# Row products and value rounds of a product-key expert layer dealt anew over the stages of a two-layer decoder step

## The reference, cut to what matters

```python
for li in range(2):                       # layer 0: RWKV-7 time mixing, layer 1: gated linear attention
    x = x + gt1 * mixer(rmsnorm(x) * (1 + sc1) + sh1)
    h = rmsnorm(x) * (1 + sc2) + sh2
    x = x + gt2 * peer(h)                 # product-key experts
...
def block(xt):                            # peer, for every token
    q = (xt @ wq).reshape(PEER_BLOCK, PEER_HEADS, 2, PEER_HALF)
    s = jnp.einsum('thpk,hpnk->thpn', q, subkeys)
    ...                                   # the 16 best of 128 keys on each side, then the 16 best of their 256 sums
    ue = jnp.take(u, expert, axis=0)      # 8 heads x 16 experts: 128 rows of 1024 numbers for every token
    act = gelu(jnp.einsum('thed,td->the', ue, xt))
    ve = jnp.take(v, expert, axis=0)
    return jnp.einsum('the,thed->td', gate * act, ve)
```

## Time and profile before

| | |
|---|---|
| time, three runs | 3379.37, 3380.48 (median), 3386.27 us |
| profiled execution | 3384.7 us, its span 3382.9 us |
| granted TensorE clock | 0.748 of full |
| TensorE matmul busy | 1900.9 us, 56% |
| VectorE busy | 1643.6 us, 49% |
| GpSimd busy | 1318.5 us, 39% |
| ScalarE busy | 267.7 us, 8% |
| HBM read | 816.05 MB, 244 GB/s over the span |

### The profile page before, as it was taken

One profiled execution on the slowest core, in us unless ns is written; L12 is line 12 of the kernel. 1 busy time (PEld: TensorE's weight loads), 2 busy tenths in 40 slices (PEclk: granted clock), 3 DMA queues, 4 the chain that ended last, 5 costly groups with the idle time before them and its releaser, 6 DMA issues.

```text
span 3382.9 us, 24243 instructions
## 1 busy us (share of the span) xinstructions
PE 1900.9 (56%) x8947; PEld 1081.7 (32%) x8947; DVE 1643.6 (49%) x3011; ACT 267.7 (8%) x422; POOL 1318.5 (39%) x1160
## 2 busy tenths in 40 slices
PE   4889648457786244565756576456255771004426
PEld 1377523125553212332314333443223360000002
DVE  3354486771221868752312522677943158880033
ACT  1111000100000000010000010011110000000000
POOL 0000026663332066433402620057664224775564
PEclk8989869578777666677878787778578885556668
DMA  7421349996567289657856943379789655998897
GB/s 240 172 92 53 129 161 397 340 339 231 187 199 261 102 324 321 217 174 253 303 190 259 392 159 129 118 269 360 262 307 357 232 193 189 355 342 309 305 312 256
DMA packets 296706, 827.99 MB, mean 245 GB/s; under 512 B 45951, under 2 KB 57135, under 8 KB 296589
## 3 DMA queue, kind: packets, MB, share of 16 engines
q0 software_dynamic: 165888, 604.05, 50.1%
q1 hardware_dynamic: 120132, 218.02, 18.4%
q10 hardware_dynamic: 10568, 4.38, 0.5%
HBM read 816.05 MB, written 10.31 MB: 244 GB/s over the span
## 4 chain that ended last, share of the span: by engine, by line
PE 35%; DVE 20%; DMA 20%; POOL 12%; issue 9%; ACT 2%; another core or an unknown queue 1%; SPq 1%; DVEq 0%; ACTq 0%; POOLq 0%; PEldq 0%
PE psum L1663 33%; POOL arena L583 12%; DVE arena L908 6%; DMA arena<-in_peer_v,idx_v 5%; DVE arena L925 4%; DMA arena<-in_peer_u,idx_u 4%; DMA wring<-in_gla_w_in 3%; DMA wring<-in_ada_w 2%; DMA wring<-in_rw_wo 1%; DVE arena L1043 1%; DVE arena L1046 1%; DVE arena L1044 1%; ACT arena L624 1%; DMA hT<-in_state_rwkv_S 1%
## 5 line engine op out<-in xcount | busy, mean ns | idle before, releaser
L583 POOL DMA_INDIRECT arena<-in_peer_u,idx_u x576 | 748.9, 1300 | 1089.1 <-DVEq L1478 617.2
L1663 PE MATMUL psum<-arena 128*32 128x512 f32 (+5 forms) x4226 | 819.0, 589 | 466.0 <-DMA arena<-in_peer_v,idx_v 160.5
L925 DVE CUSTOM_DVE_ANT_0 arena<-arena,hc 128x1024 f32<-128x1024 f32 x576 | 689.4, 1224 | 397.0 <-DMA arena<-in_peer_u,idx_u 351.8
L583 POOL DMA_INDIRECT arena<-in_peer_v,idx_v x512 | 502.7, 982 | 839.0 <-PE psum L1663 711.3
L1663 PEld LDWEIGHTS psum<-arena 128*128 128x128 f32 (+2 forms) x4226 | 397.0, 174 | 830.8 <-issue 585.6
L1663 PE MATMUL psum<-wring,cT 128*9 128x512 f32 x384 | 196.0, 671 | 129.4 <-DMA wring<-in_ada_w 128.5
L1663 PE MATMUL psum<-hT,wring 128*128 128x128 f32 (+3 forms) x1824 | 233.9, 291 | 22.6 <-DMA wring<-in_gla_w_in 14.3
L1663 PE MATMUL psum<-wring,hT 128*128 128x512 f32 x384 | 189.8, 656 | 87.5 <-DMA wring<-in_rw_wo 40.4
L1663 PEld LDWEIGHTS psum<-hT,wring 128*128 128x128 f32 (+1 forms) x1824 | 223.2, 196 | 40.9 <-issue 20.5
L624 ACT ACTIVATE arena<-psum 128x512 f32<-128x512 f32 (+5 forms) x143 | 109.2, 764 | 1248.9 <-PE psum L1663 951.7
L1663 PE MATMUL psum<-wring,arena 128*128 128x512 f32 (+1 forms) x312 | 149.5, 636 | 36.8 <-DMA wring<-in_rw_g 17.3
(11 more groups left out here) (195 smaller groups left out, 1528.9 us busy)
## 6 DMA issues: line engine op xcount, KB each, us to landing
wring<-in_ada_w SPq DMA_DIRECT2D x24, 2048.0 KB
wring<-in_peer_wq SPq DMA_DIRECT2D x20, 2048.0 KB
wring<-in_rw_w_rkv SPq DMA_DIRECT2D x12, 2048.0 KB
wring<-in_gla_w_in SPq DMA_DIRECT2D x12, 2048.0 KB
wring<-in_rw_wo SPq DMA_DIRECT2D x6, 2048.0 KB
vring<-mod_d SPq DMA_DIRECT2D x22, 512.0 KB
arena<-in_peer_u,idx_u POOLq DMA_INDIRECT x576
arena<-in_peer_v,idx_v POOLq DMA_INDIRECT x512
```

Source lines behind the costliest of these rows:

```text
L583: pool.indirect_dma_start(ring[:, s, :], None, v_rows if side else u_rows, bass.IndirectOffsetOnAxis(index, 0)).then_inc(rows_landed[s], 16)
L925: dve.tensor_tensor_reduce(ring[:, s, :], ring[:, s, :], hc[:, t, :], 1.0, 0.0, MUL, ADD, acts[:, (3 * li + t) % 2, col:col + 1]).then_inc ...
L1663: return nc.tensor.matmul(out, lhsT, rhs, start=start, stop=stop)
```

## The change

The deal of the expert work over the stages is changed; no arithmetic is.

- TensorE: `serve()` is taken out of `for_vector` and `for_scalar`; it stays in `operands()`, with higher rates (4 rounds a wait, 1.1 in `gla(0)`). In `out`, up to 6 and 4 rounds are put ahead of the two waits for chosen experts. `rest_values` at the end of `out` is kept in layer 1 alone.
- Phase 00: 28 u rows in `mix((1,2))` at its two places (rate 14), 12 after it (`rest_rows(24)`), 24 in the head of `core(1)`; the other 64 in `core(1)`'s halves (1.9 a place). `weights_due` of the first half moves into `core(1)`, that of the second to its end, and the value rounds open after that: 4 at the wait for `stateT`, 4 ahead of `turn(y)`, 4, 6 and 4 in `out(0,(1,))`, and the last 10 ahead of the first `modulation` of `core(2)`.
- Phase 01: 64 u rows in each half of `core(2)` (2.6 a place); value rounds from the end of `core(2)` on: 4, 4 and 4 at waits up to `gla_mixer((0,))`, 12 in `gla(0)`, 8 after it. `add_experts(0, 1)` moves behind `gla(0)`.
- Phase 02: u rows in `out(1,(0,))` (7 a place), `weights_due` between the first two key blocks and the first `choose`, value rounds ahead of the waits for chosen experts.
- Phase 10: u rows 6 at the norm's wait, then as before up to 64, and the other 64 at 1.6 a place in `gla(1)` and `gla(2)`; the value rounds open after `gla(2)`: 4, 6, 4, and 18 at the end of `out(1,(1,2))`.
- SyncE's loads of the gate vector (`mod_vec(0, 5)`) move with `add_experts`.

```diff
                 if t:
                     if sample:
-                        mod_vec(0, 5)
                         sp.wait_ge(region_free, w.next(region_free))
...
                 if sample:
+                    mod_vec(0, 5)
                     for hh in range(2):
...
+            RATES = {"mix": 14, "core1": 1.9, "core2": 2.6, "enter": 6, "gla": 1.6, "out": 7}
...
-                if t:
-                    weights_due(0, t - 1, 1 if t == 1 else 0)
+                if t == 1:
+                    weights_due(0, 0, 0)
+                    open_rows(0, 0, 64, 64, RATES["core1"])
                 if sample:
-                    open_rows(0, 1, 64, 64, 3.2)
+                    add_experts(0, 0, zz)
+                    open_rows(0, 1, 0, 64, RATES["core2"])
...
-                weights_due(*((0, SAMPLE) if tiles[0] == 0 else (1, 0, 0)))
-                if tiles[0]:
-                    open_rows(1, 0, 64, 64, 2.2)
+                    weights_due(1, 0, 0)
+                    open_rows(1, 0, 64, 64, RATES["gla"])
                 for t in tiles:
                     gla(t, tiles)
-                    if t == 1:
-                        weights_due(1, 0, 1)
+                if tiles[0]:
+                    weights_due(1, 0, 1)
+                else:
+                    add_experts(0, 1, add_tmp)
...
+                if li and tiles[0] == 0:
+                    open_rows(0, SAMPLE, 0, SHORT, RATES["out"])
...
+                    if li and t == 0 and half == 0:
+                        weights_due(0, SAMPLE)
...
-            open_rows(0, 0, 0, 64, 20)
+            open_rows(0, 0, 0, 64, RATES["mix"])
             mix((1, SAMPLE))
-            weights_due(0, 0, 0)
-            open_rows(0, 0, 64, 64, 8)
+            rest_rows(24)
...
+            VALUE_RATES = {"out": 4, "gla": 1.1}
...
             def for_vector():
-                serve()
...
             def for_scalar(cols=D):
-                serve()
...
                 for _ in PREP_MODS[t]:
+                    if sample:
+                        rest_values()
                     modulation()
...
                 if t == 1:
+                    fan_weights(0, 0, 1)
+                    banks.two = False
+                    open_values(0, 0, VALUE_RATES["out"])
                     operands()
...
                 if tiles[0] < SAMPLE:
                     for half in range(2):
+                        for _ in range(min(stream.left, 6 - 2 * half)):
+                            stream.left -= 1
+                            value_round()
                         pe.wait_ge(operand_written, w.next(operand_written))
                         fan_out(e1[:, 64 * half:64 * half + 64], 64)
-                rest_values()
+                if li:
+                    rest_values()
```

More of the change, by code:

```diff
@@ L520, in _ @@
                     vec(row("gla_gnorm"))
+                if tiles[0] == 0:
+                    mod_vec(0, 5)
                 if tiles[0]:
@@ L730, in core @@
                     if not group[0]:
-                        if t:
-                            weights_due(0, t - 1, 1 if t == 1 else 0)
                         if t == 1:
-                            banks.two = False
+                            weights_due(0, 0, 0)
                         for li, k in PREP_MODS[t]:
@@ L764, in core @@
                             nst[i] += 16
-                    if hh == 0:
-                        weights_due(0, 1, 1)
+                    weights_due(0, 1, hh)
                     for i in range(2):
@@ L770, in core @@
                 if t == 1:
+                    weights_due(0, 0, 1)
+                    banks.two = False
                     copy_out(state_out[0][0:RK, :], D, RK)
@@ L791, in out @@
                 t = tiles[0]
+                if li and t == 0:
+                    weights_due(0, SAMPLE, 0)
                 for half in (range(2) if t < SAMPLE else ()):
@@ L854, in gla_mixer @@
                 act.sem_inc(scalar_result, 1)
-                weights_due(*((0, SAMPLE, 0) if tiles[0] == 0 else (1, 0, 0)))
+                if tiles[0]:
+                    weights_due(1, 0, 0)
                 for t in tiles:
                     gla(t, tiles)
-                    if t == 1:
-                        weights_due(1, 0, 1)
+                if tiles[0]:
+                    weights_due(1, 0, 1)
             act.wait_ge(small_loaded, w.next(small_loaded, 64))
@@ L1275, in core @@
                         dve.sem_inc(spread_idle, 1)
-                        weights_due(0, 1, 1)
+                    weights_due(0, 1, hh)
+                    if hh == 0:
+                        open_rows(0, 1, 64, 64, RATES["core2"])
                     dve.wait_ge(scalar_result, w.next(scalar_result))
@@ L1615, in open_values, with value_rate @@
                 stream.open(fetches_of(t) // GRP, rate)
+            def value_rate(rate):
+                stream.rate = rate
             def serve(work=1.0):
@@ L1806, in core @@
                     marks = [turn_half(hh) for hh in group]
-                    if t and not group[0]:
-                        fan_weights(0, t - 1, 1 if t == 1 else 0)
-                        if t == 1:
-                            banks.two = False
-                            open_values(0, 0, 0.38)
+                    if t == 1 and not group[0]:
+                        fan_weights(0, 0, 0)
                     if not sample:
@@ L1931, in core @@
                         last.then_inc(psum_for_scalar, 1)
-                    if hh == 0:
-                        fan_weights(0, 1, 1)
-                        open_values(0, 1, 0.55)
+                    fan_weights(0, 1, hh)
+                if sample:
+                    open_values(0, 1, VALUE_RATES["out"])
                 if t == 1:
+                    fan_weights(0, 0, 1)
+                    banks.two = False
+                    open_values(0, 0, VALUE_RATES["out"])
                     operands()
@@ L2037, in gla_mixer @@
                 scalar_copies()
-                if t0 == 0:
-                    open_values(0, SAMPLE, 0.35)
+                if t0:
+                    fan_weights(1, 0, 0)
                 else:
-                    fan_weights(1, 0, 0)
+                    value_rate(VALUE_RATES["gla"])
                 for t in tiles:
                     gla(t, tiles)
-                    if t == 1:
-                        fan_weights(1, 0, 1)
-                        open_values(1, 0, 0.65)
+                if t0:
+                    fan_weights(1, 0, 1)
+                    open_values(1, 0, VALUE_RATES["out"])
+                else:
+                    rest_values()
             def out(li, tiles):
@@ L2113, in _ @@
             mix((1, SAMPLE))
-            fan_weights(0, 0, 0)
             for t in (1, SAMPLE):
```

15 lines of the change are left out of this document (7 added, 8 removed).

## The result

The changed kernel takes 3456.1 us (median of four runs, 3450.2 to 3462.4), the kernel before 3381.2 beside it (3379.4 to 3386.3): a ratio of 1.021, 95% interval 1.0185 to 1.0235. It is slower by 75 us; I had predicted 36. The profiled execution of the changed kernel took 3450.2 us, its span 3448.4, so 65.5 us of the 75 can be followed in the two traces.

The account below looks back on a forecast made before the run. No single bound, but a chain of dependent steps shared between TensorE, VectorE, transfers and GpSimd. Stage terms from -56 to +90 summed to +36 on the profiled 3384.7 us: 3420.7, or 3416 against the median; range 3338 to 3462.

Parts of the forecast that it names:

- the price of a burst: Wherever n value rounds stand together: 4 + 6.8 (n - 2) us, 17 for four, 31 for six, 58 for ten.
- the clock falls: Rival: products in `core(1)`'s halves and `gla(2)` at half clock, -26 for -50 and -42 for -56; 3454 us; chance 0.16.
- `mix((1,2))` and the head: Up to `core(1)`'s `attention`: VectorE done before `fan_weights`, -24, and shorter weight waits, -10; -35 us in all.
- `core(1)`'s halves: Level cycles without value rounds fall from 13.3 to 9.6 us at a kept 0.78 clock; -50 us, bounds -68 and -26.
- `core(1)`'s end and `out(0,(1,))`: Bursts ahead of `stateT`, +22, `turn(y)`, +2, and at the norm, +10, among others; +29 us, bounds 0 and +45.
- `core(2)`'s head: Ten rounds, 58 us, ahead of the first weight's product, less an earlier pack and shorter weights; +25 us, bounds +5 and +40.
- `core(2)`'s halves: First half stays VectorE's, second becomes like it, 172 plus 14 against 184, and a further `weights_due` is 4; +6 us.
- `gla_mixer((1,2))`: Rows ahead of the norm +7, `gla(1)` -33, `gla(2)` -22, output weights without gathers beside them -8; -56 us.
- The last stretch: Output product to phase 11's first gather: bursts and deals to 183 us, then 18 uncovered rounds, 299 for 209; +90 us.
- The tail: From phase 11's first gather to the end: left alone by the change, 0 us, within 5 us of before.
- The freed chain gains more: Rival: a round between products costs more than its own time; cycles fall to 7.8, 3358 or 3335 us; chance 0.31.
- The waits for operands are no waits: Rival: TensorE comes late to `operands()`, so rounds are simply added; `core(1)`'s end +45, `core(2)`'s head +40; 3447 us; chance 0.10.

## Why the prediction was half right

The direction was right, and the measured loss is twice the forecast: 75 us for 36. The step that failed is a size: **the price of a burst**, 4 + 6.8 (n - 2) us, and with it one burst that the sum left out. The price took the refill of the ring at its steady pace, which holds (pairs of rounds every 14 us in `core(2)`'s head; the 18 rounds at the end in 116 us, where I had 122 less 6), and it left out three things. A full ring refills only when a buffer is used, and the first refilled round can start 10.1 us after the issue of its first gather; with other loads beside it, it is up to 13.6; and some rounds run at half clock (3.4 to 3.6 us for 1.9). For four rounds that makes 19 and 23 us without other loads and 27 to 29.5 with them, in place of 17, for ten 66 in place of 58. Against the sum, the bursts ahead of `turn(y)` and at the norm in `out(0,(1,))` cost about 10 us more each, the ten rounds 6, and the burst at the norm's wait in `out(1,(1,2))`, 29.5 us, stood in no term.

That the time is still inside the range, 6 us from its upper edge, is in part luck: that edge came from the rival "the clock falls", which holds for 10 us only, and the gains of other stages, 36 us more than I gave them, hide half of the 65 us that the losses had too little.

Two of the signs that I named for being right came otherwise (the gather of phase 11 at 2911 for 2870, and 116 us for 122), and one of those for being wrong came true: the tail is 11 us off, where I allowed 5.

Point by point:

- *`mix((1,2))` and the head, -50 for -35.* The head's first weight is multiplied at 602.65 (630 before), 28 us for the 24 that I gave it, and the waits for the other three are 36 us in place of 46, as I had put them. Missing was the wait behind the last weight, for `weights_due` on VectorE: 5.0 us where it was 13.3.

```profile
602.65 8.56 PE L1675 MATMUL psum<-wring,cT 128*9 128x512 f32 x16
629.80 8.64 PE L1675 MATMUL psum<-wring,cT 128*9 128x512 f32 x16 [18.59 <-DMA wring<-in_ada_w]
647.38 8.38 PE L1675 MATMUL psum<-wring,cT 128*9 128x512 f32 x16 [8.93 <-DMA wring<-in_ada_w]
663.95 8.63 PE L1675 MATMUL psum<-wring,cT 128*9 128x512 f32 x16 [8.19 <-DMA wring<-in_ada_w]
679.83 1.97 PE L1675 MATMUL psum<-acts,pick 128*128 128x64 f32 x8 [5.01 <-DVEq L1073]
```

- *`core(1)`'s halves, -40 for -50.* The cycle is 10.1 us for the 9.6 that I took. I had kept the clock of 0.78, and it fell to 0.64 and 0.68. The mechanism of the rival "the clock falls" is real, with 10 of the 24 us that it put on these halves. With a granted 0.81 or more the cycle can be 7.4, under my lower bound of 7.8.
- *`core(1)`'s end and `out(0,(1,))`, +53 for +29.* The burst ahead of `turn(y)`, which I had laid under the load of the output weights at 2 us net, ends at 992, and the output product begins at 994 with ScalarE as its last wait. From the end of the weight's product ahead of the burst to the output product it takes 31.3 us, where in the kernel before, with one round there, it took 19.1 and ended with a wait for these weights:

```profile
1047.64 15.75 PE L1663 MATMUL psum<-wring,hT 128*128 128x512 f32 x32 [15.69 <-DMA wring<-in_rw_wo]
```

So the load would cover a burst of 17 us, and with the one of 28.8 the way to the output product is 12 us longer. The burst at the norm costs 10 more than I gave it.
- *`core(2)`'s head, +40 for +25.* 6 us are the ten rounds (65.7 for the 58 and 2 that I gave them). 14 are the pack: I had it 7 us earlier, and its first product comes 22.2 us after the stage's first load, 15.5 before, so 7 later. Its last transfer takes 15.3 us where it took 10.4; eight gathers that fill the ring, the last issued at 1144.1, are on their way beside it, which is the likely cause. The weights and what follows them gave 5 more than I had.
- *`core(2)`'s halves, -10 for +6.* From attention to attention the first half takes 179 us (188 before), the second 169 to its end (171), where I had the first unchanged and the second 2 longer, and `weights_due` on top. Taking the rounds out was worth a little more than I gave, and this is the one sign that I had wrong.
- *`gla_mixer((1,2))`, -66 for -56.* In `gla(2)` the clock did fall, to 0.71 (0.80 before), but the stretch was still shorter than I had it, so the rival's second term, 14 us of loss, isn't to be seen.

```profile
2481.00:2589.00 108.00, 51.94 (x191) 41.73 (x190) 74.77 (x103) 16.23 (x25) 33.38 (x26) 0.71 0.70 235
```

- *The last stretch, +113 for +90.* Not the 18 rounds: I had left out the burst of four at the norm's wait, 29.5 us from 2618.9 to 2648.4. The deal of the last weights ends 208 us after the output product, where I had 183.
- *The tail, -11 for 0.* It did shrink, since in the kernel before VectorE takes phase 11's first row at 2846.46, 12.3 us after the first gather, and in the changed kernel at 2916.67, 5.8 after it. Before, VectorE was still at the choice of experts and the sum behind it. That is 6 of the 11 us.

"The freed chain gains more" was right in part: in the halves a cycle without rounds can be 7.4 us, but not in this kernel, whose clock is too low for it. "The waits for operands are no waits" came nearest of all in the numbers: it put `core(1)`'s end at +45, `core(2)`'s head at +40 and the kernel at 3447, 9 us short, where +53, +40 and 3456 were measured. Its mechanism holds in part. With two rounds at the same place, the product behind them still waited 3.4 us for VectorE at the norm, but not at all ahead of `turn(y)`, where the wait came behind it and for the weights. There is a wait at most places, and it is shorter than four rounds with their gathers.

Open are the u rows of phase 11, whose pace differs by some 7 us between kernels without a reason that I found, and how much of the 10 us between the medians' difference (75) and the spans' (65.5) is anything but the spread of the runs.

## What to carry to other kernels

Work that needs gathers should be put into another engine's program one ring's worth at a time, spread out; a burst over the ring's depth pays the whole way from a freed buffer to a landed gather, and more where other loads run beside it; a burst made smaller only moved its rest to the end here. Take that way from a trace for itself, apart from the pace of a ring that runs. Before wide products are taken out of a chain of narrow ones, look at the granted clock: it may fall with them, and then a cheap one in each idle gap can be worth its time.

## What the hardware showed

- The granted clock doesn't follow TensorE's busy share alone. In `core(1)`'s halves it was 0.64 to 0.68 with TensorE busy for 178 of 226 us and never idle for more than about 1.2 us in a level, and 0.81 and 0.82 with 20 products of 128x512 more; the halves became 25 and 26 us shorter in two kernels. In the kernel before, with nearly the same busy share in its halves (213 of 266 us), it was 0.78.
- A group of four gathers (512 KB each), issued into a ring whose buffers had just come free, was complete 10.1 us after its first issue with nothing loaded beside the gathers (8.7 us of wait for TensorE, in two bursts), and 13.6 us after it with 4 MB of weights and other loads beside it (12.1 us of wait; 11.8 with an eighth of these weights). In a ring that runs, a group comes every 7 us.
